# A weight unit split behind each leading group, and the norm's root and spread moved up, in a two-block layer kernel on one core

## What is computed

```python
def first_block(x, ...):
    for l in range(DEPTH):
        x = layer_norm(ALPHA * x + 0.5 * swiglu(x, ffn1_w_gu[l], ffn1_w_down[l]), ln1_g[l], ln1_b[l])
        x = layer_norm(ALPHA * x + hybrid_mixer(x, w_in[l], ...), ln2_g[l], ln2_b[l])
        x = layer_norm(ALPHA * x + 0.5 * swiglu(x, ffn2_w_gu[l], ffn2_w_down[l]), ln3_g[l], ln3_b[l])
    return x

def second_block(x, mem, positions, ...):
    h = x
    for l in range(DEPTH):
        u = rms_norm(h, g_mix_pre[l])
        u = mlstm_rglru_mixer(u, ...) if l % 2 == 0 else sliding_window_sink_attention(u, positions, ...)
        h = h + rms_norm(u, g_mix_post[l])
        u = memory_cross_attention(rms_norm(h, g_x_pre[l]), mem, g_mem[l], w_xq[l], w_xkv[l], w_xo[l])
        h = h + rms_norm(u, g_x_post[l])
        u = squared_relu_mlp(rms_norm(h, g_ff_pre[l]), w_ff1[l], w_ff2[l])
        h = h + rms_norm(u, g_ff_post[l])
    return h
```

## Time and profile before

| | |
|---|---|
| three runs | 3457.78, 3462.31, 3464.84 us; median 3462.31 |
| the profiled execution | 3463.37 us, of which the span of instructions 3461.6 |
| mean granted TensorE clock | 0.993 of full |
| TensorE (PE) busy | 3365.1 us, 97% |
| VectorE (DVE) busy | 1781.2 us, 51% |
| ScalarE (ACT) busy | 1336.4 us, 39% |
| read from memory | 299.52 MB, 87 GB/s over the span |

### The profile page before, as it was taken

How to read it: one execution, slowest core, us unless ns; L and a number is a source line. 1 busy time by engine, 2 the same in 40 slices (tenths; PEclk the granted TensorE clock), 3 DMA queues, 4 the chain that set the end, 5 groups by cost and what they waited for, 6 DMA issues and landing times.

```text
span 3461.6 us, 38145 instructions
## 1 busy us (share of the span) xinstructions
PE 3365.1 (97%) x15606; PEld 2754.0 (80%) x15606; DVE 1781.2 (51%) x2710; ACT 1336.4 (39%) x2120; POOL 62.4 (2%) x65
## 2 busy tenths in 40 slices
PE   9999989999999999899999999999999989999999
PEld 7888767888888887778888778777888778778887
DVE  4333785433463337854434774546443765655443
ACT  3222654322242225543322554434322565444222
POOL 0000100000000000000000000000000000000000
PEclk9999999999999999999999999999999999999999
DMA  5333311333333323113333233222333313213332
GB/s 160 96 96 88 82 49 55 107 97 95 96 91 96 96 89 82 49 55 112 106 95 95 80 97 104 79 61 79 101 98 98 80 55 94 72 55 110 98 97 67
DMA packets 604286, 304.10 MB, mean 88 GB/s; under 512 B 43600, under 2 KB 601808, under 8 KB 603984
## 3 DMA queue, kind: packets, MB, share of 16 engines
q1 hardware_dynamic: 604112, 301.66, 30.4%
HBM read 299.52 MB, written 2.10 MB: 87 GB/s over the span
## 4 chain that ended last, share of the span: by engine, by line
PE 78%; DVE 12%; ACT 7%; issue 1%; DMA 1%; SPq 0%; DVEq 0%; ACTq 0%
PE ps L1707 24%; PE ps L1708 24%; PE ps L1715 24%; DVE wl L2112 2%; ACT wh L1889 1%; DVE tmp L2121 1%; DVE Y L2287 1%; PE ps L1776 1%; PE ps L1858 1%; PE ps L1874 1%; DVE XR L2210 1%; DVE XL L2196 1%; ACT XH L1939 1%; PE ps L1761 1%; ACT tmp L1966 1%
## 5 line engine op out<-in xcount | busy, mean ns | idle before, releaser
L1707 PE MATMUL ps<-XH,wh 128*128 128x512 f32 (+1 forms) x2624 | 1047.1, 400 | 22.2 <-DVE wl L2112 13.1
L1715 PE MATMUL ps<-XL,wh 128*128 128x512 f32 (+1 forms) x2856 | 1062.0, 382 | 0.5 <-DVE XL L2188 0.5
L1708 PE MATMUL ps<-XH,wl 128*128 128x512 f32 (+1 forms) x2624 | 1019.6, 389 | 0.0
L2112 DVE TENSOR_TENSOR wl<-raw,wh 128x1024 fp32r<-128x1024 f32 (+1 forms) x565 | 680.5, 1210 | 517.1 <-ACT wh L1889 517.0
L1889 ACT ACTIVATE wh<-raw 128x1024 fp32r<-128x1024 f32 (+1 forms) x565 | 584.2, 1039 | 557.0 <-PE ps L1715 487.2
L1715 PEld LDWEIGHTS ps<-XL,wh 128*128 128x128 f32 x2856 | 538.5, 189 | 105.2 <-DVE XL L2188 1.1
L1707 PEld LDWEIGHTS ps<-XH,wh 128*128 128x128 f32 x2624 | 495.6, 189 | 141.7 <-DVE wl L2112 19.0
L1708 PEld LDWEIGHTS ps<-XH,wl 128*128 128x128 f32 x2624 | 495.7, 189 | 100.4 <-issue 3.4
L1707 PE MATMUL ps<-HHa,wh 128*128 128x512 f32 x1088 | 429.5, 395 | 10.1 <-DVE HLa L2116 5.7
L1708 PE MATMUL ps<-HHa,wl 128*128 128x512 f32 x1088 | 424.5, 390 | 0.0
L1715 PE MATMUL ps<-HLa,wh 128*128 128x512 f32 x1088 | 408.7, 390 | 0.0
(11 more groups left out here) (331 smaller groups left out, 3080.3 us busy)
## 6 DMA issues: line engine op xcount, KB each, us to landing
raw<-in_ffn_w_gu SPq DMA_DIRECT2D x176, 512.0 KB, 3.8
raw<-in_w_ff SPq DMA_DIRECT2D x128, 512.0 KB, 4.1
raw<-in_ffn_w_down SPq DMA_DIRECT2D x64, 512.0 KB, 4.0
raw<-in_w_xkv SPq DMA_DIRECT2D x32, 512.0 KB, 3.9
raw<-in_ev_w_in SPq DMA_DIRECT2D x25, 512.0 KB, 3.9
raw<-in_ffn_w_down SPq DMA_DIRECT2D x32, 384.0 KB, 3.3
raw<-in_w_in SPq DMA_DIRECT2D x24, 512.0 KB, 3.9
raw<-in_w_out SPq DMA_DIRECT2D x64, 128.0 KB, 2.8
```

What stands on the lines that cost most here:

```text
L1707: e.matmul(bank[:, c], t.wh[u % SPL][:, k, :], h[:, c], start=first, stop=False, skip_group_check=True)
L1708: e.matmul(bank[:, c], t.wl[u % SPL][:, k, :], h[:, c], start=False, stop=False, skip_group_check=True)
L1715: m = e.matmul(bank[:, 0:n], t.wh[u % SPL][:, k, :], l, start=False, stop=last, skip_group_check=True)
L2112: self.e.tensor_tensor(wl, raw, f32(wh), ALU.subtract).then_inc(self.s["lo"], self.tag("lo", f"lo.{i}"))
```

## The change

`split_to` is taken out of `next_unit` as a function of its own. `start` calls it once behind the leading group, so that unit 4 is split there, ahead of everything that the caller writes next. In `pre_scale`, the root and its reciprocal are written before unit 4 is asked for (and so ahead of the split of unit 7), and the spread and its copy become a filler of unit 4: `spread` is advanced after each input tile, does nothing at the first and writes the spread at the second.

```diff
         if self.units_in is None:
             self.units.append((*w, k0, nk, c0))
             return i
-        n = len(self.units_in)
-        while self.n_split < min(n, base + SPL):
+        self.split_to(base + SPL)
+        return i
+
+    def split_to(self, limit):
+        n = len(self.units_in or ())
+        while self.n_split < min(n, limit):
             while self.n_loaded < min(n, self.n_split + RAW):
                 self.load_unit(self.n_loaded)
                 self.n_loaded += 1
@@
         while self.n_loaded < min(n, self.n_split + RAW):
             self.load_unit(self.n_loaded)
             self.n_loaded += 1
-        return i
@@ def stream
         def start(order=None, lead=LEAD):
             got.extend(self.project_group(todo[:lead], xs, 0, order, self.parts))
             self.parts = None
+            self.split_to(self.u + 2)
@@ def pre_scale
         nxt.ahead()
         steps = self.stats.finish_steps(D, RMS_EPS)
         next(steps)
+        next(steps)
+        got = []
+
+        def spread():
+            yield
+            try:
+                next(steps)
+            except StopIteration as r:
+                (rb, rt), = r.value
+            rr, f = self.tmp.take()
+            k = self.copy_act(rr[:, :], rb[:, :], rt, f)
+            self.psum.give(rb, k)
+            got.extend((rr, k))
+
+        self.fill_with(spread(), 1)
         nxt.ahead()
-        next(steps)
-        try:
-            next(steps)
-        except StopIteration as r:
-            (rb, rt), = r.value
-        rr, f = self.tmp.take()
-        k = self.copy_act(rr[:, :], rb[:, :], rt, f)
-        self.psum.give(rb, k)
-        return rr, k
+        self.drain()
+        return got
```

## The result

The changed kernel takes **3442.53 us** (median of 4 runs, 3441.97 to 3443.79). Against runs of the kernel before the estimated ratio is 0.9941, 95% interval 0.9929 to 0.9953: 0.59% faster, some 20 us, with an interval of 16 to 25. The forecast was 13.8 us: right in sign and in which waits go, 6 to 7 us short, and its term for the clock is the one that failed. The time lies inside the stated range.

The account below looks back on a forecast made before the run. TensorE, at work 97% of the span, bounds the kernel, so only its waits count; 5.3 + 0.6 - 0.2 + 3.8 + 2.65 + 1.6 = 13.75 us won gives 3448.5 us against the median, range 3440 to 3457.

Parts of the forecast that it names:

- term for the clock: At mixer2's lru product, full clock without the standstill: 2.24 instead of 3.6 us, 1.4 us won.
- Output projections, 5.3: At six output projections unit 4's first matmul no longer waits for `wl`: 4.33 idle and 6x0.16, 5.3 us won.
- mixer1, 0.6: At both mixer1 inputs the 2.38 us wait goes, but the VectorE and ScalarE path takes most back: 0.6 us won.
- Channel sums 1.1 us later: At the six RMS streams the sums start behind unit 4's low half, so channel sums come 1.1 us later on TensorE.
- The spread waits 0.3: At the six RMS streams the reciprocal is ready at 2729.9, TensorE there at 2729.65 (swa's times): 0.3 us wait.
- swa, 3.8: At swa's input the earlier factor moves the first score from 2743.12 to 2739.3: 3.8 us won, attention shifting whole.
- mixer2, 2.65: At mixer2's lru product, 1.25 us from a small weight's earlier load and 1.4 from full clock: 2.65 us won.
- ffn 0, 1.6: At ffn 0's unit 8, the positions' load lands 1.6 us sooner and half of the 3.73 wait stays: 1.6 us won.
- a rival at 0.12 and 3445.5: Waits behind ffn 0 and swa no longer bring TensorE's clock down, each drop worth some 1.5 us: 3445.5, chance 0.12.
- mixer1's gain whole: Rival: the path through mixer1 is TensorE's, both 2.54 stay won, 4.5 us more: 3444, chance 0.08.
- the head start worth nothing: Rival: small loads land when they did, ScalarE's copies hold swa's chain: 4 us won, 3458.5, no change, chance 0.12.
- the reciprocal held by unit 6's load: Rival: reciprocal behind unit 6's late-loaded half, spread waits in unit 4, six places lose about 4.1: 3481, chance 0.04.

Follow-up runs that it names:

- A alone: Changed kernel with root and spread back where they were before, keeping only unit 4's split behind the leading group: 3448.88 us, ratio 0.9964 against the kernel before.
- B alone: Changed kernel without the unit split behind the leading group, keeping only root ahead and spread between tiles: 3459.73 us, ratio 0.9991 against the kernel before.
- positions early: Changed kernel with the load of the positions issued one hidden tile ahead of their first use: 3439.00 us, ratio 0.9933 against the kernel before.

## Why the prediction was right or wrong

- **Output projections, 5.3: right**, 6.1 by the traces without the clock. All six waits went, and nothing queued behind the halves became late. The 0.16 that I added to each wait was too little: the starts of the matmuls behind give 1.30 for the idle time of 1.03, 1.63 for 1.36, 0.63 for 0.35, which is 0.27 more each. The matmul behind a wait is itself longer on record, 0.50 in the earlier trace rows where others take 0.39.
- **"The gated feed-forward starts show no such wait over 0.15 us: nothing": wrong, 1.2 us.** Unit 4's first matmul was late there too, by an idle time of 0.10, and each of three starts gave 0.40. In the kernel before, at the first of them (0.39 behind 614.71 is 615.10):

```profile
614.71 0.39 PE L1715 MATMUL ps<-XL,wh 128*128 128x512 f32 x1
615.19 0.50 PE L1707 MATMUL ps<-XH,wh 128*128 128x512 f32 x1
```

- **mixer1, 0.6: short**, 1.3. VectorE's and ScalarE's chain does bind and takes back most of the 2.54, at 402.74 and 431.00, nearer than I had looked. The slack on it was 0.67 each. I had taken VectorE's wait of 0.28 for the slack and "no larger" one, though ScalarE's 0.69 stands beside it in the earlier trace rows; that it is this 0.69 which gave way isn't shown.
- **Channel sums 1.1 us later: right**, 1.02 to 1.09 at five places and 1.30 at mixer2. **"The spread waits 0.3": wrong**, it waits for nothing. From the start of the channel sums (2713.75) the reciprocal was done after 2.31, where I had 2.4, and TensorE needed 2.39 for the sums and six matmuls (2716.14), where I had 2.15. That is 0.3 six times, and explains why cross 0, cross 1 and ffn 1 together won 0.9 instead of losing 0.2.
- **swa, 3.8: right**, 4.0 by the traces, as one chain.
- **mixer2, 2.65: two parts.** To the products 2.0 were won; sums 0.2 later than costed, and the load still 0.62 late in all. The clock there is full again, as taken.
- **ffn 0, 1.6: between the two executions, 1.0 and 2.5, and not for its reason.** The positions' load took 5.98 us instead of 4.55 and landed at 2360.65; the wait fell by 1.27, and whether the clock falls behind it differs from one execution to the next.
- **The step that failed is the term for the clock**: 1.4 us forecast, at one place. The mean clock over 9 and 32 runs gives 7.5. The step of the text was "Without the standstill I take full clock", applied to mixer2's first products and priced at nothing everywhere else, with the rest left to a rival at 0.12 and 3445.5. That rival came nearer to the measured time than the forecast. Its mechanism is right in swa (0.93 to 0.99) but named the wrong place at ffn 0, and none of it foresaw 1980, where the wait is the same 2.77 us in both kernels and the clock behind it was low in both profiles of the kernel before and full in both of the change.
- The clock rule that the prediction cited (the Trainium skill, TensorE: Matmul & The Clock Gate, "What's actually happening": looks that run freely, and a number of cold matmuls that varies from run to run) agrees with the two profiles of the change, 0.79 at 2375 in one and 1.00 in the other, behind waits of 2.46 and 2.59. It agrees with those of the kernel before as well: behind mixer1's wait at 402 the clock was 1.00 in the first (wait 2.38) and 0.67 from 403 to 407 in the second (wait 2.37).
- The other rivals: mixer1's gain whole (no, 1.3 of 5.1), the head start worth nothing (no), the reciprocal held by unit 6's load (no: that half started at 2710.78, well ahead).
- Two slips in the sums change nothing above: 23 matmuls in 5.00 us make 5.2 us for 24 and not 5.4 (the starts in the trace, 0.23 apart, do give 5.4), and the upper ends of the four terms add up to 3441 where the text has 3442.

What is left open: why the total of the low periods differs between the two kernels, how steady it is for one of them (9 runs of the change lie within 3 us, with clocks of 0.995 and 0.996; 32 of the kernel before within 11, with 0.991 to 0.996), and why equal waits at 1980 end differently. In the other variants the clock behind 1980 was full in three profiles (A alone, B alone, positions early) and low in six; no run here tells what sets it. The parts that I call clock in the table are read from PEclk and not from an experiment that changes the clock alone.

## What to carry to other kernels

An engine's half of a weight unit does two things: it makes the unit ready, and it frees the buffer for a later load. Of a split that is moved, follow the second as well, down to what is queued behind the unit that this load feeds; moving it back lengthened the waits by 3 us at swa's score and by about 2 at each use of a small load. If TensorE is the bound and its clock falls behind standstills, read (1 - PEclk) times the span first: 24 us of it were there to be read before. Give the clock a term of its own and a range at every long wait of a stage that changes, and look at what the engine would then wait for: in swa's attention 6.2 us of clock came back and 2.7 us of new waits with them. And compare where matmuls start, not only the idle time over a threshold, before calling a kind of start free.

## What the runs showed that was not expected

The low clock weighs about as much here as the waits that were removed (7.5 us over many runs, 10.1 us of waits): 11.9 to 27.8 us of it per execution among the kernels run here, all of which do the same matmuls. A standstill of the same length (2.77 us ahead of the second lru products, 2.46 and 2.59 at unit 8) was followed by the lower clock in one execution and by the full one in another. The positions' load, with one unit less queued ahead of it, let its first step start 1.9 us sooner (2358.75 and 2360.67); 0.7 of it is that the channel sums started sooner there (2349.93 and 2350.61).
